# Order of weight loads and of split work in the Strassen-like feed-forwards of a streaming encoder

## The reference

```python
def swiglu(x, w_gate, w_up, w_down):
    return (jax.nn.silu(x @ w_gate) * (x @ w_up)) @ w_down

for l in range(DEPTH):                       # DEPTH = 2
    if l == N_A_LAYERS:                      # shared keys and values of layer B
        kv = (rms_norm(x, g_kv_b) @ w_kv_b) ...
    x = x + 0.5 * swiglu(rms_norm(x, g_norm[l, 0]), w_ffn_gate[l, 0], w_ffn_up[l, 0], w_ffn_down[l, 0])
    ...                                      # differential attention (A) or forgetting attention (B)
    x = x + 0.5 * swiglu(rms_norm(x, g_norm[l, 2]), w_ffn_gate[l, 1], w_ffn_up[l, 1], w_ffn_down[l, 1])
```

## Time and profile before

| what | value |
|---|---|
| median of 3 runs | 2517.05 us (2516.7 to 2520.76) |
| the profiled execution | 2516.2 us, span 2514.0 us |
| mean granted TensorE clock | 0.992 |
| PE busy | 2413.0 us, 96% |
| DVE busy | 1859.1 us, 74% |
| ACT busy | 1338.0 us, 53% |
| POOL busy | 546.1 us, 22% |
| DMA | 334.20 MB, mean 133 GB/s |

### The profile page before, as it was taken

The page is one execution under the profiler, slowest core; times in us unless marked ns, Lnnn a source line. Parts: engine busy times, 40 slices in busy tenths (PEclk is TensorE's granted clock), DMA queues, the critical chain, the costliest instruction groups (busy, mean ns, idle before and its releaser), DMA issues. The chain is left out here.

```text
span 2514.0 us, 48940 instructions
## 1 busy us (share of the span) xinstructions
PE 2413.0 (96%) x18377; PEld 2267.6 (90%) x18377; DVE 1859.1 (74%) x3710; ACT 1338.0 (53%) x2870; POOL 546.1 (22%) x421
## 2 busy tenths in 40 slices
PE   8899999999998999999999999999999999999998
PEld 7899999788678999999988889999996699999998
DVE  7887979422687888787935889787928878787865
ACT  6555556201785655555622555555618856555554
POOL 0222122344000122222135122222131001222210
PEclk9999999999999999999999999999999999999999
DMA  5656565232763465756434665666457644666652
GB/s 133 122 116 139 108 139 105 88 117 85 282 241 108 93 122 112 141 119 133 94 84 138 172 130 111 138 125 129 99 210 255 224 117 78 138 116 138 124 112 82
DMA packets 419397, 334.20 MB, mean 133 GB/s; under 512 B 20641, under 2 KB 379738, under 8 KB 418914
## 3 DMA queue, kind: packets, MB, share of 16 engines
q1 hardware_dynamic: 279376, 246.98, 31.8%
q0 software_dynamic: 133136, 65.82, 21.4%
q10 hardware_dynamic: 6658, 18.37, 2.0%
HBM read 314.98 MB, written 16.13 MB: 132 GB/s over the span
## 5 line engine op out<-in xcount | busy, mean ns | idle before, releaser
L925 PE MATMUL PS<-x_area,w_area 128*128 128x320 f32 x3096 | 482.2, 309 | 0.0
L925 PEld LDWEIGHTS PS<-x_area,w_area 128*128 128x128 f32 x3096 | 461.1, 188 | 0.3 <-DVE w_area L2276 0.3
L2276 DVE TENSOR_TENSOR w_area<-R,w_area 128x512 fp32r<-128x512 f32 (+2 forms) x583 | 357.1, 617 | 119.1 <-ACT w_area L1638 118.3
L1638 ACT ACTIVATE w_area<-R 128x512 fp32r<-128x512 f32 (+2 forms) x583 | 324.8, 567 | 223.3 <-PE PS L925 88.6
L2276 DVE TENSOR_TENSOR r_area<-R,r_area 128x512 fp32r<-128x512 f32 (+2 forms) x437 | 270.6, 620 | 115.4 <-ACT r_area L1638 105.0
L925 PE MATMUL PS<-r_area,w_area 128*128 128x320 f32 x1584 | 271.2, 314 | 25.1 <-ACT PS L1723 17.1
L1638 ACT ACTIVATE r_area<-R 128x512 fp32r<-128x512 f32 (+2 forms) x437 | 248.0, 568 | 60.6 <-DVE R L2297 40.2
L925 PEld LDWEIGHTS PS<-r_area,w_area 128*128 128x128 f32 x1584 | 243.1, 191 | 32.9 <-ACT PS L1723 29.8
L1723 ACT ACTIVATE PS<-PS 128x320 f32<-128x320 f32 x438 | 179.8, 417 | 160.0 <-PE PS L925 143.7
L1148 PE MATMUL PS<-w_area,xn_hi 128*128 128x512 f32 x800 | 252.4, 397 | 4.9 <-POOL w_area L769 3.6
L925 PE MATMUL PS<-r_area 128*128 128x320 f32 x1392 | 238.4, 311 | 8.4 <-ACT PS L1723 6.0
(11 more groups left out here) (341 smaller groups left out, 4169.6 us busy)
## 6 DMA issues: line engine op xcount, KB each, us to landing
R<-in_w_ffn_up_dram SPq DMA_DIRECT2D x45, 512.0 KB, 5.3
R<-in_w_ffn_gate_dram SPq DMA_DIRECT2D x43, 512.0 KB, 5.4
R<-in_w_ffn_up_dram SPq DMA_DIRECT2D x86, 256.0 KB, 3.7
R<-in_w_ffn_up_dram POOLq DMA_DIRECT2D x86, 256.0 KB, 4.7
R<-in_w_ffn_gate_dram SPq DMA_DIRECT2D x82, 256.0 KB, 4.6
R<-in_w_ffn_gate_dram POOLq DMA_DIRECT2D x81, 256.0 KB, 4.9
R<-in_w_ffn_down_dram SPq DMA_DIRECT2D x52, 384.0 KB, 3.8
R<-in_w_ffn_down_dram SPq DMA_DIRECT2D x88, 192.0 KB, 3.2
```

Source lines behind the costliest of these rows:

```text
L925: last = pe.matmul(PS[:, bank, 0:HT], a[:, k, :], b, start=(start and opens), stop=(k == n - 1 and a is lo), skip_group_check=True)
L1638: act.activation(role_parts(f, g, s, role)[0], role_source(f, g, s, role), ACT.Copy).then_inc(sem("early_cast") if key in EARLY_COUNT else ...
L2276: dve.tensor_tensor(lo, role_source(f, g, s, role), hi.bitcast(F32), ALU.subtract).then_inc(sem("early_split") if key in EARLY_COUNT else ...
```

## The change

It has five parts. (1) In an opening, ACT does copy 1 ahead of hidden "5", and S3's cast and copy 2 ahead of the casts of then.W11, S4 and hidden "4"; DVE does S3's low part ahead of theirs; `splits` has S3 ahead there. (2) SP issues the S1 quarter of set k+1 before the W11 quarter and the half of set k. (3) At seams the first two (square) or four (row) tiles wait for their own place only, and the calls of `finish_one` and `tile_high` at the end of a feed-forward stand in another order. (4) The hidden parts of f0's first pair are made after its first set, on ACT and DVE. (5) The store of the turned keys is issued after the first set of f2, with a semaphore of its own, for which the hidden parts of f2's pair 1 wait (those of pair 0 wait for the store of the values). Two small semaphores are merged into one.

```diff
@@ splits
+        third = [(at, "S3")] if at != order[0] else []
+        out += third if opens_down(*at) else []
+        out += ([(then, "W11")] if then else []) + [(at, "S4")] + (third if not opens_down(*at) else [])
-        out += ([(then, "W11")] if then else []) + [(at, "S4")] + ([(at, "S3")] if at != order[0] else [])
@@ SP
-            def quarter_load(f, g, s):
+            def first_quarter(f, g, s):
+                key = f, g, s
                 if PLAN.raw_free[key, 3]:
                     sp.wait_ge(w_split, PLAN.raw_free[key, 3])
                 if PLAN.landed3[key] > 16:
                     sp.wait_ge(w_loaded3, PLAN.landed3[key] - 16)
                 sp.dma_start(role_source(*key, "S1"), weight_block(*key, 0, 1)).then_inc(w_loaded3, 16)
+            def other_quarters(f, g, s):
+                key, p = (f, g, s), LOAD[f, g, s] % 2
                 if PLAN.raw_free[key, 1]:
                     sp.wait_ge(w_split, PLAN.raw_free[key, 1])
                 sp.dma_start(role_source(*key, "W11"), weight_block(*key, 0, 0)).then_inc(w_loaded[p], 16)
                 set_load(f, g, s, (1,))
@@ SP, load_ffn
-                for g, s in chain(f):
-                    if set_at(f, g, s) is not early:
-                        quarter_load(f, g, s)
+                sets = [(f, *at) for at in chain(f) if set_at(f, *at) is not early]
+                first_quarter(*sets[0])
+                for key, then in zip(sets, sets[1:] + [None]):
+                    if then is not None:
+                        first_quarter(*then)
+                    other_quarters(*key)
@@ SP, load_square (free is None) and load_rows
+            def opening_tile(name, j, view, src):
+                sp.wait_ge(w_split, PLAN.raw_free[name, j])
+                sp.dma_start(view, src).then_inc(w_loaded[LOAD[name, j] % 2], 16)
@@ SP, before B's attention
-            sp.wait_ge(stored, STORED["kt"])
+            sp.wait_ge(stored, STORED["bv"])
+            sp.wait_ge(sem("kt_stored"), 16)
@@ ACT, opening_down
                 hidden_rows(f, *prev, "1")
+                copy_rows(f, *cur, 1)
                 hidden_rows(f, *prev, "5")
-                copy_rows(f, *cur, 1)
                 hidden_rows(f, *prev, "7")
                 hidden_rows(f, *prev, "2")
+                role_high(f, *cur, "S3")
+                copy_rows(f, *cur, 2)
                 role_high(f, *then, "W11")
                 role_high(f, *cur, "S4")
                 hidden_rows(f, *prev, "4")
-                role_high(f, *cur, "S3")
                 role_high(f, *then, "S1")
-                copy_rows(f, *cur, 2)
                 role_high(f, *then, "S2")
@@ ACT, ffn
-                    for k in range(2):
-                        tile_high(name, k)
-                        finish_one(KB - 2 + k)
+                    tile_high(name, 0)
+                    finish_one(KB - 3)
+                    tile_high(name, 1)
+                    for k in range(KB - 2, KB):
+                        finish_one(k)
@@ ACT, f0's first pair; DVE has its counterpart first_hidden_parts
-            for part in HIDDEN_PARTS[1:]:
-                first_hidden_cast(part)
-            ffn(0, None, partial(finish_tile, 0, 0, 0, 1), "qkv")
+            def first_hidden_casts():
+                for part in HIDDEN_PARTS[1:]:
+                    first_hidden_cast(part)
+            ffn(0, None, partial(finish_tile, 0, 0, 0, 1), "qkv", first_hidden_casts)
@@ ACT, before f2
-            act.wait_ge(sem("heads_read"), 30)
-            act.dma_start(k_scr, kT[:, :, :].rearrange("p h t -> p (h t)")).then_inc(stored, 16)
-            ffn(2, None, partial(finish_tile, 2, 3, 2, 4), "qb")
+            def store_keys():
+                act.wait_ge(sem("heads_read"), 30)
+                act.dma_start(k_scr, kT[:, :, :].rearrange("p h t -> p (h t)")).then_inc(sem("kt_stored"), 16)
+            ffn(2, None, partial(finish_tile, 2, 3, 2, 4), "qb", store_keys)
@@ ACT and DVE, hidden parts of f2, group 0 (k is the pair)
-                        act.wait_ge(stored, STORED["kt"])
+                        act.wait_ge(*((sem("kt_stored"), 16) if k else (stored, STORED["bv"])))
@@ DVE, opening_down
+                role_low(f, *cur, "S3")
                 role_low(f, *then, "W11")
                 role_low(f, *cur, "S4")
                 hidden_lows(f, *prev, "4")
-                role_low(f, *cur, "S3")
@@ ACT and DVE, ffn_sets
+                    if n == 0 and after_first is not None:
+                        after_first()
                     if finish_one is not None and cur[0] == len(GROUPS) - 1 and is_down(*cur):
                         tiles = 2 * (cur[1] - width(cur[0]) - 1)
                         finish_one(tiles)
-                        finish_one(tiles + 1)
+                        if then is not None:
+                            finish_one(tiles + 1)
```

More of the change, by code:

```diff
@@ L635, in load_square @@
                 base, s, first = BASE[name], SLOT[name], 0
-                if free is not None:
+                if free is None:
+                    first = 1
+                    for u in range(2):
+                        opening_tile(name, u, *cols(w, (s + u) % 2, u * P))
+                else:
                     first = 2
@@ L650, in load_square, with row_tile, load_opening_rows, load_rows @@
                     tile(base + m * 2 + 1, 1 - s, *cols(w, 1 - s, m * 2 * P + P))
-            def load_rows(w, base, par, n_tiles, first=0):
-                with sp.Fori(0, n_tiles) as n:
+            def opening_tile(name, j, view, src):
+                sp.wait_ge(w_split, PLAN.raw_free[name, j])
+                sp.dma_start(view, src).then_inc(w_loaded[LOAD[name, j] % 2], 16)
+            def row_tile(w, s, u, at):
+                return (raw[s][:, 0:1024].rearrange("p (k m) -> p k m", k=2),
+                        w[u * 256:(u + 1) * 256, bass.ds(at, 512)].rearrange("(k p) m -> p k m", p=P))
+            def load_opening_rows(w, name, column):
+                for u in range(4):
+                    opening_tile(name, u, *row_tile(w, (SLOT[name] + u) % 2, u, column * 512))
+            def load_rows(w, base, par, n_tiles, first=0, done=0):
+                with sp.Fori(done, n_tiles) as n:
                     for u in range(4):
                         s = (par + u) % 2
-                        tile(base + n * 4 + u, s, raw[s][:, 0:1024].rearrange("p (k m) -> p k m", k=2),
-                             w[u * 256:(u + 1) * 256, bass.ds(n * 512 + first * 512, 512)].rearrange("(k p) m -> p k m", p=P))
+                        tile(base + n * 4 + u, s, *row_tile(w, s, u, n * 512 + first * 512))
             def load_attention(x, vc, f_scr):
@@ L1795, in opening_down, with ffn_sets @@
                 role_high(f, *then, "W12")
-            def ffn_sets(f, mean=None, finish_one=None):
+            def ffn_sets(f, mean=None, finish_one=None, after_first=None):
                 order = chain(f)
@@ L2139, in _ @@
             act.wait_ge(sem("lam_sums"), 2)
[L2140 removed]
+            act.activation(small[:, 4:6], small[:, 6:8], ACT.Exp).then_inc(sem("small_exps"), 1)
             act.preload_act_table_set("natural_log_exp_and_others")
@@ L2166, in _ @@
             act.wait_ge(step, count.next())
-            act.activation(lf1, lf2, ACT.Ln, bias=1.0).then_inc(sem("ln_ready"), 1)
+            act.activation(lf1, lf2, ACT.Ln, bias=1.0).then_inc(sem("small_exps"), 1)
             act.wait_ge(sem("rows_read"), 8 * TB + 2)
@@ L2572, in opening_down, with ffn_sets @@
                 role_low(f, *then, "W12")
-            def ffn_sets(f, root, finish_one=None):
+            def ffn_sets(f, root, finish_one=None, after_first=None):
                 order = chain(f)
@@ L2633, in ffn_sets, with ffn @@
                         finish_one(tiles)
-                        finish_one(tiles + 1)
-            def ffn(f, root, event, version, g_next, name=None):
+                        if then is not None:
+                            finish_one(tiles + 1)
+            def ffn(f, root, event, version, g_next, name=None, after_first=None):
                 def finish_one(k):
@@ L2643, in ffn @@
                 if name is not None:
-                    ffn_sets(f, root, finish_one)
+                    ffn_sets(f, root, finish_one, after_first)
                     tile_low(name, 0)
+                    finish_one(KB - 3)
                     sums_out(f, *last)
```

40 lines of the change are left out of this document (20 added, 20 removed).

## The result

The changed kernel takes 2650.95 us (median of 4, 2650.8 to 2652.18), the kernel before 2518.91 us in the same comparison: ratio 1.0524, 95% interval 1.0505 to 1.0542. The profiled execution took 2652.2 us against 2516.2, 136 us more. The prediction had the sign, the place and, for the gate/up sets, the mechanism, but 54 us where 132 were measured; the time lies above its range.

A forecast was written before the change was run, and what follows sets the result against it. The prediction took TensorE, busy 96% of the span, to bound the kernel. It added 43.5 us for 11 groups net of the openings' gain, 19 for depth 2 and −8.5 for the rest to 2516.2, giving 2570 us, range 2495 to 2612.

The forecast's parts named there:

- Part 1's price: Openings of down sets: S3's product comes 1.36 us sooner in each of 11 with depth 3, −15.0 us if kept.
- The ring's formula: Gate/up sets: two sets take 17.7 + 2L us, L being the W11 quarter's issue to landing; break-even L = 3.46.
- Its S3 product is back at its old place: Down set behind an opening: the late W11 quarter gives back the opening's 1.36 us, no more.
- Nothing waits for it within the opening: Openings: S2's low part of the next set ends 0.75 us later, at no cost within the opening.
- I take 4.4, with 3.9 and 5.0 as the ends: W11 quarter's landing time in us in gate/up sets: +43.5 us over 11 groups, +10 and +83 at the ends.
- the prediction's own upper case: Gate/up sets of 11 groups with the W11 quarter landing in 5.0 us: +83 us.
- Group 0, +19: Groups of depth 2: late W11 quarters cost 15.0 us in down sets and 4.2 in gate/up pairs, together +19 (5 to 30).
- The key store, −3.5 with +4 as its other end: Start of f2: moving the store behind the first set saves 3.5 us of a 5.8 us gap, bounds −5.8 and +4.
- The seams: Three seams to square and row weights: earlier tile loads and casts remove 1.3 us each, −4 us together.
- The first pair: f0's first pair, hidden parts made behind the first set: −1 us, bounds −3.5 and +2.
- Rival B: Heavier DMA traffic, W11 quarters landing in 5.0 us: 2615 us, chance 0.11.
- Rival A: W11 quarters land in time, under 3.46 us in gate/up sets, so the new order does no harm: 2491 us, chance 0.24.

The follow-up runs named there:

- e1: The changed kernel with SP's old order of loads (S1 quarter, W11 quarter and half of one set, then the next set): 2508.51 us, ratio 0.995.
- e3: The changed kernel with a third SP order (W11 quarter of set k, S1 quarter of set k+1, half of set k): 2483.26 us, ratio 0.9856.
- e2: The kernel before with only the change's new order of loads on SP: 2651.55 us, ratio 1.0524.
- e9: e3 with the store of the turned keys back at its old place, ahead of f2's sets: 2485.81 us, ratio 0.9887.
- e8: e3 with ScalarE's copies of partial sums ahead of its second finishing step in the last group's down sets: 2479.41 us, ratio 0.9856.
- e12: e3 with e8's copies first and the key store behind f2's second set, f0's first pair as in the kernel before: 2476.77 us, ratio 0.9832.
- e13: The changed kernel with the third role's accumulating DMA held back until the next W11 quarter has landed: 2694.96 us, ratio 1.0708.
- e4: The changed kernel with the W11 quarter still waiting for S2's low part, but issued ahead of the S1 quarter: 2554.22 us, ratio 1.0136.

## Why the prediction was wrong in size

**Right.** *Part 1's price.* −1.36 us per opening was measured, as the mean of all 11 in each of two kernels (e1, e3). *What decides.* The W11 quarter behind the S1 quarter, issued when S2's low part is done, was named as the cause, and e1 and e2 show it from both sides. *The ring's formula.* Between the S3 products at 272.72 and 300.33 two W11 quarters are issued, at 275.20 and 287.37, and they land in 4.6 and 5.3 us (gate and up quarter). 17.7 + 2L is then 27.6 us; measured 27.61.

**Wrong, in order of size.**

*"Its S3 product is back at its old place".* I worked the ring out for gate/up sets and for depth 2, and for the down sets of depth 3 only took the opening's 1.36 us as given back. This is the largest step that failed. That ring is 1.61 (S3's to S2's low) + 0.44 + L + 1.12 + 1.73 = 4.9 + L, by the timeline of the changed kernel, so its break-even against 9.24 is L = 4.3, and L was 4.1 to 5.9 in all but one of f0's, so near it or above it. The three down sets behind an opening lose 4.1 us in each group, 45.5 in all, and the openings keep 9.5 of their gain: 36 us net where the sum had 0. Part 1 adds to it: what was moved behind S3 in the opening lets S2's low of the next set end 3.4 us after the opening's S3 product (204.89 against 201.49), where it was 1.5 before, and the next quarter is issued later by that. The first down set behind an opening loses 2.0 us in the changed kernel and 0.1 in e2. "Nothing waits for it within the opening" was true, and the next set's quarter did. The openings in turn kept less than in e1, where they gained 15.0: in f0's groups 1 to 3 PE waits 0.8 to 1.1 us for hidden "7" before S2's last block, where e1 has 0.56.

*"I take 4.4, with 3.9 and 5.0 as the ends".* This term of the sum was too small, and is the second. The median was 5.1 in gate/up and down sets together between 210 and 490 us, and 5.2 in the 84 quarters of gate/up sets. Both burdens were named. I took a value below that of the earlier trace rows, where a quarter had only one of them (4.6 and 5.1); the row nearest to the new case was the upper bound, and with both burdens the landing came out there or above. With L = 5.0, the mean of the two landings above, the formula gives the prediction's own upper case, 83 us for 11 groups where it took 43.5; measured 77.5 over groups 1 to 3.

*Group 0, +19.* It was +34.8, of which 4.8 are the first gap of f2. The down sets of depth 2 lose 16 us, where the sum had 15.0. The gate/up sets of this group lose 19, where it had 4.2: this term was mis-sized, and no run here takes apart why these sets lose so much more.

*The clock* had no term, and in gate/up sets none was missing. In the changed kernel the third set of a group has a gap of 2.5 us, and the one behind it, with no gap at all, takes 1.63 us more than before since its first matmuls ran at the lower level. PE's busy time is 38.9 us higher than before for the same matmuls. But that is time which PE would else have stood: the ring sets when the fifth set's S3 product can start, and its gap is shorter by what the slow matmuls took. e2 shows both cases. In f1's group 2 the clock stays up behind the third set's stall, in f2's group 2 it falls (columns as in the view by stretch above):

```profile
1116.50:1120.40 3.90, 3.87 (x26) 3.87 (x27) 3.76 (x8) 2.89 (x6) 1.28 (x1) 1.00 0.26 34
1709.10:1713.00 3.90, 3.85 (x16) 3.85 (x17) 3.76 (x8) 2.88 (x7) 1.28 (x1) 0.57 0.30 38
```

and the fifth set's S3 products begin with

```profile
1144.03 2.02 PE L932 MATMUL PS<-v_area,w_area 128*128 128x320 f32 x12 [2.52 <-ACT PS L1730]
...
1737.06 1.14 PE L932 MATMUL PS<-r_area,w_area 128*128 128x320 f32 x6 [1.50 <-ACT PS L1730]
```

From the third S3 product of a group to the fifth the seven groups of e2 in which the clock stays up take 27.5 to 29.1 us (median 27.8), the four in which it falls 27.5 to 29.5 (median 27.9).

*The key store, −3.5 with +4 as its other end.* It was +4.8 in the changed kernel, since the W11 quarter there took 12.9 us. With early quarters the gap is the same, 5.8 us before and 5.9 in e3, for the collision is with the third role's sum, which the store meets at both places (it lands in 13.4 and 13.5 us). The ratios of e3 and e9 leave room for a gain of some us, which no trace shows.

*The other parts.* The seams each lose 1.1 us of wait, 0.10 being left of 0.57 and 0.65, about as forecast (1.3), but the last groups' copies take it back (e8). The first pair: nothing (e12).

In sum the prediction had 43.5 us for groups 1 to 3, 19 for group 0 and −8.5 for the rest; the columns of the table are 77.5 and 36, 34.8, and −12. Rival B had the right cause, a heavier L, and 2615 us: what it lacked is above all the ring of the down sets. Rival A, the order without harm, has its time measured in e1: 2508.5 where it said 2491. That was too low by what the down sets behind the openings, group 0 and the gate/up sets give back (8.0, 6.2 and 6.2 us in the table). The Trainium skill's rule of arbitration ("DMA: Bandwidth & Descriptors", "Queues, rings and completion order") fits e13: without the accumulating DMA beside it the quarter lands in 3.4 us, with it in 5.1. By its fit of 2.0 us + bytes / 436e3 ("Anatomy of one DMA — SWDGE (gpsimd) path"), which it states for DMAs that GpSimd issues, the second of two quarters would by estimate land in 2.7 us. No kernel with late quarters reached that in the median: with the accumulating DMA held back it was 3.4 us.

What stays open is the 0.4 us of landing that e4 saves against the changed kernel: whether the S1 quarter ahead, or less traffic on the other queues, makes them.

## What to carry to other kernels

Issue loads in one queue in the order in which their places come free: a wait at the head of a queue delays all that stands behind it, and here one swap of two lines cost 5.2%, and the right order of the same loads gained 0.7%. When a load is moved to a later event, write down the ring that it closes, for each kind of step, with its fixed part, its landing time and the pace of the bound engine; near break-even, small terms decide. Take the landing time from the rows with the most traffic beside, not from their median. Where such a ring sets the pace, don't add the slow matmuls behind a stall to the stalls: look first whether they only fill time in which the engine would have waited.

## What the runs showed of the hardware that I had not expected

An accumulating DMA of 256 KB beside it makes a plain load of 256 KB land in 5.2 us in place of 3.4 (median of the 84 W11 quarters of gate/up sets, the changed kernel and e13), and it suffers itself, from 4.6 to 5.6 us in the median of the third role's sums of gate/up sets. Beside a store of 2.6 MB the sum took 13.7 us.

The lower clock came after some short stalls and not after others of the same length. Of the 20 stalls of over 2.4 us that PE has before a feed-forward product in the changed kernel, 14 are followed by matmuls at 0.18 to 0.28 us each over the next twelve, where 0.15 is normal. Of the ten between 1.7 and 2.4 us four are, and of the 14 between 1.4 and 1.7 us none. In the change's gate/up sets this cost little or nothing, as the two groups of e2 above show.
